# The norms of a two-layer hybrid block: reciprocals of rows instead of wide tiles

## The reference

```python
def rmsnorm(x, w):
    xf = x.astype(jnp.float32)
    y = xf * lax.rsqrt(jnp.mean(xf * xf, axis=-1, keepdims=True) + EPS)
    return (y * w.astype(jnp.float32)).astype(x.dtype)

for layer in range(DEPTH):
    hl = rmsnorm(x, norm_mix_w[layer]) * (1.0 + sc1) + sh1
    hc = rmsnorm(xc, norm_mix_w[layer]) * (1.0 + scc1) + shc1
    y_l, y_c = mixer(hc, hl, ...)
    x = x + g1 * y_l
    x = x + g2 * swiglu(rmsnorm(x, norm_ffn_w[layer]) * (1.0 + sc2) + sh2,
                        w_ffn_in[layer], w_ffn_out[layer])
    ...
return rmsnorm(x, final_norm_w)
```

## Time and profile before

| | us |
|---|---|
| median of 3 runs | 4011.81 |
| lowest, highest | 4010.82, 4022.57 |
| profiled execution, its own time | 4001.74 |
| its span | 4000.0 |

### The profile page before, as it was taken

How to read it: one execution, slowest core, us unless ns; L and a number is a source line. 1 busy time by engine, 2 the same in 40 slices (tenths; PEclk the granted TensorE clock), 3 DMA queues, 4 the chain that set the end, 5 groups by cost and what they waited for, 6 DMA issues and landing times. The chain is left out here.

```text
span 4000.0 us, 56996 instructions
## 1 busy us (share of the span) xinstructions
PE 3450.5 (86%) x21948; PEld 2871.5 (72%) x21948; DVE 1583.2 (40%) x2599; ACT 1064.0 (27%) x1947; POOL 650.9 (16%) x734
## 2 busy tenths in 40 slices
PE   5989756958698999999998989656877879999998
PEld 2778645846686888888886778545756758888885
DVE  3465744622315223223235466644622242322334
ACT  2343124621204121211213343124512131221112
POOL 1133643212100000000001133642222000000000
PEclk8999878978698999999999999878987989999999
DMA  4456273088200111111111456373195111111111
GB/s 164 138 185 190 86 218 107 22 237 254 105 26 29 39 37 37 42 37 37 37 41 73 138 187 190 87 225 95 27 292 173 42 42 47 47 47 52 47 47 58
DMA packets 275838, 398.78 MB, mean 100 GB/s; under 512 B 107715, under 2 KB 181187, under 8 KB 274886
## 3 DMA queue, kind: packets, MB, share of 16 engines
q1 hardware_dynamic: 272134, 385.84, 31.1%
q0 software_dynamic: 3520, 10.49, 0.7%
HBM read 280.02 MB, written 104.15 MB: 96 GB/s over the span
## 5 line engine op out<-in xcount | busy, mean ns | idle before, releaser
L901 PE MATMUL ffn_bank<-ffn_h_hi,ffn_w_hi 128*128 128x512 f32 (+1 forms) x1760 | 650.2, 369 | 18.1 <-DVE ffn_h_lo L314 18.1
L904 PE MATMUL ffn_bank<-ffn_h_lo,ffn_w_hi 128*128 128x512 f32 (+1 forms) x1760 | 649.5, 369 | 0.0
L905 PE MATMUL ffn_bank<-ffn_h_hi,ffn_w_lo 128*128 128x512 f32 (+1 forms) x1760 | 649.0, 369 | 0.0
L811 PE MATMUL frt_acc<-frt_w_hi,frt_h_hi 128*128 128x472 f32 x960 | 375.8, 391 | 47.3 <-DVE frt_w_lo L688 26.2
L901 PEld LDWEIGHTS ffn_bank<-ffn_h_hi,ffn_w_hi 128*128 128x128 f32 x1760 | 333.1, 189 | 75.9 <-DVE ffn_h_lo L314 18.1
L904 PEld LDWEIGHTS ffn_bank<-ffn_h_lo,ffn_w_hi 128*128 128x128 f32 x1760 | 333.1, 189 | 55.3
L905 PEld LDWEIGHTS ffn_bank<-ffn_h_hi,ffn_w_lo 128*128 128x128 f32 x1760 | 332.8, 189 | 55.5
L811 PE MATMUL frt_acc<-frt_w_hi,frt_h_lo 128*128 128x472 f32 x960 | 368.2, 384 | 0.0
L811 PE MATMUL frt_acc<-frt_w_lo,frt_h_hi 128*128 128x472 f32 x960 | 365.6, 381 | 0.0
L895 DVE TENSOR_TENSOR ffn_w_lo<-ffn_raw,ffn_w_hi 128x1024 fp32r<-128x1024 f32 x132 | 161.8, 1226 | 502.8 <-ACT ffn_w_hi L891 497.6
L901 PE MATMUL ffn_bank<-ffn_a_hi,ffn_w_hi 128*128 128x512 f32 (+1 forms) x880 | 324.2, 368 | 0.8 <-DVE ffn_a_lo L969 0.8
(11 more groups left out here) (309 smaller groups left out, 5543.6 us busy)
## 6 DMA issues: line engine op xcount, KB each, us to landing
ffn_raw<-w_ffn SPq DMA_DIRECT2D x132, 512.0 KB, 3.4
x<-ada_w SPq DMA_DIRECT2D x20, 2048.0 KB, 11.0
proj<-frt_out SPq DMA_DIRECT2D x120, 236.0 KB, 2.0
x<-proj SPq DMA_DIRECT2D x60, 384.0 KB, 4.6
frt_raw<-w_in SPq DMA_DIRECT2D x96, 236.0 KB, 4.4
pack<-frt_side SPq DMA_DIRECT2D x80, 256.0 KB, 2.5
scn_fd<-feat SPq DMA_DIRECT2D x40, 384.0 KB, 7.6
met_pr<-proj SPq DMA_DIRECT2D x20, 704.0 KB, 5.6
```

What stands on the lines that cost most here:

```text
L811: mm = pe.matmul(acc[q % NA][:, 0:GW], a[:, k, tok], b[:, k, :], start=(k == 0 and i == 0), stop=(k == KC - 1 and i == 2))
L901: mm = pe.matmul(out, w_hi, b_hi, start=first, stop=False)
L904: pe.matmul(out, w_hi, b_lo, start=False, stop=False)
L905: return pe.matmul(out, w_lo, b_hi, start=False, stop=last)
```

## The change

All five norms are changed in the same way. The sums stay as they are, with the mean squares in every partition. Then, for a slice of n columns:

1. ScalarE copies one row of the sums (1 x n) from PSUM into `line`.
2. TensorE turns it by one small product for each tile of 128 columns (four, or two for 256 columns): the piece of the row is the weight, a 1 x 2 piece of a constant matrix the moving operand. Column t of the tile's tokens then stands down the partitions.
3. ScalarE takes the root of two equal numbers a tile, eight in a row, VectorE the reciprocal of eight.
4. TensorE spreads them: for each tile one product with the reciprocals, repeated over 128 columns, as the weight and the unit matrix as the moving operand. The result lies in the PSUM tile `ms` again, over the sums.
5. VectorE's scalings read it there, instead of the tile `inv` in SBUF.

The order is changed too. ScalarE issues two squares of the next slice ahead of each of the first four roundings, the row copy ahead of the fifth and the root ahead of the sixth. VectorE takes the next slice's reciprocal behind its seventh scaling, and the first scaling of the next slice stands ahead of the last rest of this one. On TensorE turning and spreading stand right behind the slice's sums. In the ffn stages `sil` serves as buffer for the squares.

```diff
@@ -242,17 +242,17 @@
                 m.gpsimd_end(pool)
 
 
-def normed(nc, st, x, scale, mod, shift0, lo, hi_t, lo_t, ones, eps, bufs=None, ms=None):
+def normed(nc, st, x, scale, mod, shift0, lo, hi_t, lo_t, ones, mats, eps, bufs, ms):
 
 
     slices = token_slices(lo)
-    if bufs is None:
-        bufs = ([st.sb(f"sq{u}", [P, 512])[:] for u in range(2)], [st.sb(f"scaled{u}", [P, 512])[:] for u in range(2)],
-                [st.sb(f"inv{s}", [P, n])[:] for s, (t0, n) in enumerate(slices)])
-        ms = [st.ps(f"ms{s}", [P, 512]) for s in range(len(slices))]
-    sq, scaled, inv = bufs
-    squared, summed, rooted, inverted = st.sem("squared"), st.sem("summed"), st.sem("rooted"), st.sem("inverted")
+    NS = len(slices)
+    sq, scaled = bufs
+    line = [st.sb(f"line{s}", [1, 512]) for s in range(NS)]
+    root, rstd = [[st.sb(f"{n}{s}", [P, 4, 2]) for s in range(NS)] for n in ("root", "rstd")]
+    squared, summed, lined, turned_s, rooted, inverted, spread = [st.sem(n) for n in ("squared", "summed", "lined", "turned_s", "rooted", "inverted", "spread")]
     scaled_s, rounded, h_ready = st.sem("scaled"), st.sem("rounded"), st.sem("h_ready")
+    unit, ident = mats[0:1, C_LE, 0:2], mats[:, C_ID, :]
 
     def act_norm(act, between=None):
         def square(s, k):
@@ -262,9 +262,15 @@
                 act.wait_ge(summed, i - 1)
             act.activation(sq[i % 2][:, 0:n], x[:, k, t0:t0 + n], ACT.Square).then_inc(squared, 1)
 
-        def root(s):
+        def take_line(s):
+            n = slices[s][1]
             act.wait_ge(summed, (s + 1) * KC)
-            act.activation(inv[s], ms[s][:, 0:slices[s][1]], ACT.Sqrt, bias=eps[:]).then_inc(rooted, 1)
+            act.activation(line[s][:, 0:n], ms[s][0:1, 0:n], ACT.Copy).then_inc(lined, 1)
+
+        def take_root(s):
+            tiles = slices[s][1] // P
+            act.wait_ge(turned_s, s + 1)
+            act.activation(root[s][:, 0:tiles, :].rearrange("p t n -> p (t n)"), ms[s][:, 0:2 * tiles], ACT.Sqrt, bias=eps[:]).then_inc(rooted, 1)
 
         def round_(s, k):
             t0, n = slices[s]
@@ -275,35 +281,54 @@
 
         for k in range(KC):
             square(0, k)
-        root(0)
+        take_line(0)
+        take_root(0)
         if between:
             between(act)
-        for s in range(len(slices)):
+        for s in range(NS):
             for k in range(KC):
-                if s + 1 < len(slices):
-                    square(s + 1, k)
+                if s + 1 < NS:
+                    if k < KC // 2:
+                        square(s + 1, 2 * k)
+                        square(s + 1, 2 * k + 1)
+                    if k == KC // 2:
+                        take_line(s + 1)
+                    if k == KC // 2 + 1:
+                        take_root(s + 1)
                 round_(s, k)
-            if s + 1 < len(slices):
-                root(s + 1)
 
     def pe_sum(pe, s):
         t0, n = slices[s]
         for k in range(KC):
             pe.wait_ge(squared, s * KC + k + 1)
             pe.matmul(ms[s][:, 0:n], ones[:], sq[(s * KC + k) % 2][:, 0:n], start=(k == 0), stop=(k == KC - 1)).then_inc(summed, 1)
+        pe.wait_ge(lined, s + 1)
+        for t in range(n // P):
+            mm = pe.matmul(ms[s][:, 2 * t:2 * t + 2], line[s][:, t * P:(t + 1) * P], unit, start=True, stop=True)
+        mm.then_inc(turned_s, 1)
+
+    def pe_spread(pe, s):
+        t0, n = slices[s]
+        pe.wait_ge(inverted, s + 1)
+        for t in range(n // P):
+            mm = pe.matmul(ms[s][:, t * P:(t + 1) * P], rstd[s][:, t, 0:1].broadcast_to([P, P]), ident, start=True, stop=True)
+        mm.then_inc(spread, 1)
 
     def dve_norm(dve):
+        def invert(s):
+            tiles = slices[s][1] // P
+            dve.wait_ge(rooted, s + 1)
+            dve.reciprocal(rstd[s][:, 0:tiles, :], root[s][:, 0:tiles, :]).then_inc(inverted, 1)
+
         def scale_one(i):
             s, k = i // KC, i % KC
             t0, n = slices[s]
             v = 1 if t0 < CTX else 0
             if k == 0:
-                dve.wait_ge(rooted, s + 1)
-                dve.reciprocal(inv[s], inv[s]).then_inc(inverted, 1)
-                dve.wait_ge(inverted, s + 1)
+                dve.wait_ge(spread, s + 1)
             if i >= 2:
                 dve.wait_ge(h_ready, i - 1)
-            dve.scalar_tensor_tensor(scaled[i % 2][:, 0:n], x[:, k, t0:t0 + n], scale[:, k, v:v + 1], inv[s],
+            dve.scalar_tensor_tensor(scaled[i % 2][:, 0:n], x[:, k, t0:t0 + n], scale[:, k, v:v + 1], ms[s][:, 0:n],
                                      ALU.mult, ALU.mult).then_inc(scaled_s, 1)
 
         def rest(i):
@@ -314,18 +339,17 @@
             dve.scalar_tensor_tensor(lo_t[:, k, t0:t0 + n], scaled[i % 2][:, 0:n], mod[:, shift0 + k, v:v + 1],
                                      hi_t[:, k, t0:t0 + n].bitcast(F32), ALU.add, ALU.subtract).then_inc(h_ready, 1)
 
-        parts = len(slices) * KC
+        parts = NS * KC
+        invert(0)
         scale_one(0)
         for i in range(parts):
-            if (i + 1) % KC == 0:
-                rest(i)
-                if i + 1 < parts:
-                    scale_one(i + 1)
-            else:
+            if i + 1 < parts:
                 scale_one(i + 1)
-                rest(i)
-
-    return act_norm, pe_sum, dve_norm, h_ready
+            if i % KC == KC // 2 + 1 and i // KC + 1 < NS:
+                invert(i // KC + 1)
+            rest(i)
+
+    return act_norm, pe_sum, pe_spread, dve_norm, h_ready
 
 
 def front(nc, layer, x, x_copy, w_in, proj, mod, amix, ones, eps, conv_w, small, mats, tri, pack, feat, diag, inv, tot):
...
@@ -360,9 +384,8 @@
         slices = token_slices(0)
         sq_n = [carve("side", [512]) for _ in range(2)]
         scaled_n = [carve("side", [512]) for _ in range(2)]
-        inv_n = [carve("side", [n]) for t0, n in slices]
         taken["side"] = 0
-        act_norm, pe_sum, dve_norm, h_ready = normed(nc, st, x, amix, mod, 0, 0, h_hi, h_lo, ones, eps, (sq_n, scaled_n, inv_n), [b_s, b_D, b_g])
+        act_norm, pe_sum, pe_spread, dve_norm, h_ready = normed(nc, st, x, amix, mod, 0, 0, h_hi, h_lo, ones, mats, eps, (sq_n, scaled_n), [b_s, b_D, b_g])
 
         pr, before, after = [[carve("x", [768]) for _ in range(2)] for _ in range(3)]
         cv, cw, sq = carve("x", [768]), carve("x", [3, 768]), carve("x", [512])
@@ -905,7 +930,7 @@
     return pe.matmul(out, w_lo, b_hi, start=False, stop=last)
 
 
-def ffn(nc, layer, x, lo, units, mod, affn, ones, eps):
+def ffn(nc, layer, x, lo, units, mod, affn, ones, mats, eps):
 
 
     J = 4
@@ -1053,6 +1077,7 @@
             def _(pe):
                 for i in range(NS):
                     pe_sum(pe, i)
+                    pe_spread(pe, i)
                 with pe.Fori(0, NFULL) as g:
                     with pe.Fori(0, J) as j:
                         pe_up(pe, g * TURNS + j, g * SETS + j)
@@ -2201,15 +2226,16 @@
                         add(n, u)
 
 
-def final(nc, x, norm_w, out, ones, eps):
+def final(nc, x, norm_w, out, ones, mats, eps):
 
     with Stage(nc, "fin") as st:
         nw = st.sb("nw", [P, KC])
         sq = [st.sb(f"sq{i}", [P, 512]) for i in range(2)]
-        root, inv = st.sb("root", [P, 512]), [st.sb(f"inv{i}", [P, 512]) for i in range(2)]
+        root, rstd = [[st.sb(f"{n}{i}", [P, 4, 2]) for i in range(2)] for n in ("root", "rstd")]
+        line = [st.sb(f"line{i}", [1, 512]) for i in range(2)]
         y = st.sb("y", [P, KC, LAT])
         ms = [st.ps(f"ms{s}", [P, 512]) for s in range(2)]
-        s = signals(st, "set_in squared summed rooted inverted done stored")
+        s = signals(st, "set_in squared summed lined turned rooted inverted spread done stored")
         with nc.Block() as block:
             @block.sync
             def _(sp):
@@ -2230,15 +2256,25 @@
                             act.wait_ge(s["summed"], i - 1)
                         act.activation(sq[i % 2][:], x[:, k, t:t + 512], ACT.Square).then_inc(s["squared"], 1)
                     act.wait_ge(s["summed"], (sl + 1) * KC)
-                    if sl:
-                        act.wait_ge(s["inverted"], 1)
-                    act.activation(root[:], ms[sl][:], ACT.Sqrt, bias=eps[:]).then_inc(s["rooted"], 1)
+                    act.activation(line[sl][:], ms[sl][0:1, :], ACT.Copy).then_inc(s["lined"], 1)
+                    act.wait_ge(s["turned"], sl + 1)
+                    act.activation(root[sl][:].rearrange("p t n -> p (t n)"), ms[sl][:, 0:8], ACT.Sqrt, bias=eps[:]).then_inc(s["rooted"], 1)
 
             @block.tensor
             def _(pe):
                 for i in range(2 * KC):
                     pe.wait_ge(s["squared"], i + 1)
                     pe.matmul(ms[i // KC][:], ones[:], sq[i % 2][:], start=(i % KC == 0), stop=(i % KC == KC - 1)).then_inc(s["summed"], 1)
+                    if i % KC == KC - 1:
+                        sl = i // KC
+                        pe.wait_ge(s["lined"], sl + 1)
```

(28 more changed lines are left out.)

## The result

| | median us | runs |
|---|---|---|
| before | 4009.97 | 8 (4003.71 to 4022.57) |
| after | 4028.43 | 8 (4017.60 to 4033.10) |

The ratio is 1.0044, 95% interval 1.0029 to 1.0058: slower by 12 to 23 us, some 18 in the middle. The profiled execution took 4017.60 us (span 4015.8), 15.8 us more of span than before; it is the shortest of the eight. The forecast was 4021 us, +8.9.

The account below looks back on a forecast made before the run. TensorE, busy 86%, was taken as the bound, so norms count only where it waits for them. Five norm terms, 0.5 + 0.0 + 4.6 + 2.2 + 1.6 = +8.9 us, on the median 4011.81 gave 4021 us, range 4007 to 4034.

Parts of the forecast that it names:

- first ffn norm: Norm of the first ffn stage: start -0.1, first slice +0.8, second and last -0.2 each; +0.5 us, bounds -4 and +2.5.
- second ffn norm: Norm of the second ffn stage: start -0.75, slice +1.1 at low clock or -1.5 at high; 0.0 us, bounds -2 and +1.5.
- first front: First front stage's norm: slice 0's h +2.5 us later, projections +2.1 from the low clock; +4.6 us, bounds +1 and +7.
- second front: Second front stage's norm: slice 0's h +1.0 us, projections +1.2; +2.2 us in all, bounds 0 and +5.
- final: Final norm: slice 1's sums stand behind slice 0's spreading, chain 3.6 us instead of 4.1; +1.6 us, bounds +1 and +3.5.
- the high-clock case: Slices hosting the next slice's sums, TensorE at 2.4 GHz: 14.8 us for 512 columns, 12.1 for 256.
- the low (15.1 and 17.4): The same slices with TensorE at 1.2 GHz for two chunks: 17.4 us for 512 columns, 15.1 for 256.
- The sign that I had named: In the ffn norms a 512-column slice takes 15 to 17 us; 12.5 or less would prove the forecast wrong.
- The rival with the high clock: TensorE stays at 2.4 GHz because paired squares feed it more tightly: -3 us in all, 4009 us; chance 0.14.
- The price list: Prices of the norms' small steps, such as spreading 1.15 us, small root 0.27, reciprocal 0.20, 512-column chain 3.6 us.
- the 2 us that I had named as a sign against the list: Spreading, the eight instructions of 128 columns in a norm, was priced at 1.15 us; above 2 us would break the prices.
- The 6.7 us estimated by the Trainium skill's rule on PSUM: All 104 scalings reading one operand from PSUM: 6.7 us more by fixed costs, sum near 4027; the forecast priced it at nothing.

Follow-up runs that it names:

- weights put back: The changed kernel with the weight tiles of both ffn stages back at their addresses in the kernel before, no instruction differing: 4008.32 us, ratio to before 0.9992.

## Why the prediction came out as it did

The time lay in its range, and slower was given 0.30, but this was luck: the sum was right in sign for a wrong reason. The terms, read from the spans above (for the ffn stages with the pace taken out, for the fronts from the first square to ScalarE's second copy of a projection, for the final stage to the start of the last scalings):

| term, us | forecast | after | weights put back |
|---|---|---|---|
| first ffn norm | +0.5 | -1.9 | -0.2 |
| second ffn norm | 0.0 | -4.2 | -1.8 |
| first front | +4.6 | +2.6 | +3.1 |
| second front | +2.2 | -1.1 | -2.0 |
| final | +1.6 | +2.9 | -0.2 |
| place of the weights | 0 | +13.1 | 0 |
| sum | +8.9 | +11.4 | -1.1 |

The profiles' spans differ by 15.8 us; the other 4.4 lie in modulation, the mixers and the later part of the fronts, and are not explained. Nor is what the medians have beyond that.

- **The step that failed** is "everything outside the norms is left as it is. Two square buffers fewer in the ffn stages change nothing". I asked whether the scratch used in their place was free, and not what their going does to the tiles allocated behind them. It is the largest term, and no row of before could have priced it; but the move itself could be read from the allocations.
- **The norm's own terms** were forecast at +8.9 and were -1.7 after and -1.1 with the weights put back. Much of the difference is the clock. I expected 1.2 GHz at the head of most sums and projections, and for two chunks of a slice. Stretches after, to be laid beside the earlier trace rows:

```profile
62.90:69.40 6.50, 6.50 (x15) 2.31 (x13) 4.22 (x7) 4.24 (x8) 6.21 (x7) 0.84 0.00 0
...
76.50:81.50 5.00, 4.94 (x13) 4.18 (x14) 2.17 (x4) 0.56 (x1) 0.00 (x0) 0.50 0.00 0
...
1218.70:1233.40 14.70, 12.20 (x38) 6.18 (x39) 11.41 (x17) 10.54 (x18) 0.00 (x0) 0.85 0.01 2
...
1218.70:1221.00 2.30, 1.73 (x2) 0.84 (x3) 2.26 (x4) 1.65 (x3) 0.00 (x0) 0.51 0.01 4
1221.00:1224.00 3.00, 3.00 (x7) 1.03 (x5) 1.02 (x3) 1.93 (x4) 0.00 (x0) 0.81 0.00 0
...
114.30:118.60 4.30, 4.27 (x20) 3.80 (x21) 0.78 (x2) 0.34 (x1) 0.00 (x0) 1.00 0.81 244
...
2204.60:2208.90 4.30, 4.30 (x13) 3.66 (x14) 0.75 (x2) 0.31 (x1) 0.00 (x0) 0.60 0.81 261
```

  Counted from the first square, the first row is the place in the front where TensorE had worked 7 instructions at a granted clock of 0.50; here it is 15 at 0.84. The projections of the first front did begin at 0.50, as forecast (76.50), and the sums of the first ffn norm's second slice began at 0.51; but those were at 1.00 again from 1224.0, where before the clock was 0.50 for all of 6.3 us. Behind the release at 114.33 it was 1.00 from the first product, after a wait of 2.69 us; in the earlier trace rows the same place, after a wait of 9.84 us, stands at 0.51. Ten products took 4.1 us there and take 2.2 here. The release itself came 4.6 us late, as forecast to the tenth; 2 us of it were given back by the clock. In the second front the wait was 3.30 us, the clock behind it 0.60, and ten products took 3.6 us; there the release was not late at all, against the +2.2 forecast. In the sum I had priced what TensorE's added work costs, and not that it shortens the waits ahead of long rows of products.

  Part of the gain is no work of the change. In the second ffn norm the eight sums of the first slice, the same work in both kernels, took 7.52 us instead of 9.09, and that is half of the 3 us by which its long stretch starts earlier.
- **The slices.** VectorE's timeline of the first ffn norm after, to be laid beside the earlier trace rows:

```profile
1206.31 0.87 DVE L331 SCALAR_TENSOR_TENSOR ffn_prod<-x,affn,ffn_bank 128x256 f32<-128x256 f32 x2 [1.31 <-PE ffn_bank L314]
...
1210.26 0.48 DVE L339 SCALAR_TENSOR_TENSOR ffn_h_lo<-ffn_prod,mod,ffn_h_hi 128x256 fp32r<-128x256 f32 x1 [1.89 <-ACT ffn_h_hi L279]
...
1218.66 0.75 DVE L331 SCALAR_TENSOR_TENSOR ffn_prod<-x,affn,ffn_bank 128x512 f32<-128x512 f32 x1
...
1233.44 0.75 DVE L331 SCALAR_TENSOR_TENSOR ffn_prod<-x,affn,ffn_bank 128x512 f32<-128x512 f32 x1
```

  12.35 us for the first slice and 14.8 for the second: the values of the high-clock case (12.1 and 14.8), not of the low (15.1 and 17.4), though the clock was low at the head of both. The sign that I had named, a slice of 15 to 17 us, was just missed. VectorE does not stop at the boundaries and waits inside the slice, up to 1.95 us, as forecast. The rival with the high clock, which said -3 us in all, came nearer to the norms, but its condition did not hold in full: a low clock for a chunk cost less than I had reckoned.
- **The price list held**, but for one bound. Spreading, in the first ffn norm and in the first front:

```profile
1217.01 1.16 PE L314 MATMUL ffn_bank<-mats,ffn_rstd 128*128 128x128 f32 x8 [0.59 <-DVE ffn_rstd L321]
...
99.99 2.08 PE L314 MATMUL frt_b_g<-mats,frt_rstd 128*128 128x128 f32 x8 [1.25 <-DVE frt_rstd L321]
```

  It took 1.16 us at the high clock (forecast 1.15) and 2.08 at the low, just over the 2 us that I had named as a sign against the list. Two scalings of 256 columns with one operand in PSUM took 0.87 us, eight of 512 in the final stage 5.36 against 5.39 before. The 6.7 us estimated by the Trainium skill's rule on PSUM (VectorE: DVE Perf Modes, TRN2 errata) are not there.
- **Final stage**, the two sets of sums and the last scalings after:

```profile
3982.21 9.09 PE L2267 MATMUL fin_ms<-fin_sq,ones 128*128 128x512 f32 x16 [2.35 <-ACT fin_sq L2257]
...
3995.73 8.15 PE L2267 MATMUL fin_ms<-fin_sq,ones 128*128 128x512 f32 x16
...
4007.39 5.36 DVE L2288 SCALAR_TENSOR_TENSOR fin_y<-x,fin_nw,fin_ms 128x512 f32<-128x512 f32 x8 [1.25 <-PE fin_ms L2276]
```

  As forecast the second sums stand behind the spreading. The size hangs on the clock again. With the weights put back the two sets of sums took 7.52 and 7.42 us, and the term was -0.2 instead of +2.9. But in the kernel before the first set had taken 9.20 us, so 1.7 us of that difference are the clock in work that the change leaves alone; without them the term would be +1.5, near the forecast +1.6.

## What to carry to other kernels

A change that removes or adds a buffer moves every tile allocated behind it. Compare the starts of the weight and moving tiles of all long products before and after, and keep their distance modulo 256 bytes; if a profile shows a product of unchanged code with another mean duration and no idle time, look there first. And where an engine's in-order queue holds long work between two short pieces that another engine waits for, look at the order of that queue first: here it was worth 16 us by itself, and the shape of the short pieces nothing that the runs could tell.

## What the runs showed of the hardware

- The pace of back-to-back float32r products with a weight load each, at a granted clock of 1.00, depends on the distance between the starts of the weight and the moving tile modulo 256 bytes: 226.7 to 234.3 ns for 512 columns, 113.3 to 119.5 for 256. Moving both together changes nothing. The Trainium skill (SBUF — State Buffer, the section "Who interferes with whom") gives TensorE two independent read ports, one for the moving operand and one for weights, and says that TensorE never waits on anyone. The runs fit this as far as other engines go: with them busy or idle the pace is 232.4 or 232.3 ns. But between the kernels at 226.7 and at 232.4 ns only the place of the weights relative to the stage's other tiles differs, so for TensorE's own two operands the independence does not show.
- That the two reads collide is the likely reading, and no run shows it directly. It stays open what sets the level at each distance, whether weights of the two passes (hi and lo) could lie at different best distances, and whether the fronts' projections would gain from other places; none of this was tried.
